# Moving fill tiles around the first attention's compressed scores, and reordering the second attention's vector, scalar and closing work

## The chip, the cores and the metric

The kernel runs on one core of a Trainium2 chip. The metric is the time of one execution on the device, in microseconds (us). Three timed runs of the kernel before gave 2184.55, 2186.37 and 2181.2 us, so the median is 2184.55 us.

## The reference

The reference is two transformer blocks applied one after the other to x, a 512 x 1024 float32 matrix, with all weights in float32. What matters here is cut out:

```python
# first block: "NSA" attention beside a convolution branch
u = rmsnorm(h, g_mix);  z = u @ w_in            # queries, keys, values, gates, conv input, merge gates
kc = compress(kv[0], ...); vc = compress(kv[1], ...)     # 31 compressed keys/values per group of heads
lc = q @ kc.T;  pc = masked_softmax(lc, cmp_end <= t);  o_c = pc @ vc
o_s, o_w = ...                                  # two causal softmax attentions over all 512 keys
o = gates[0] * o_c + gates[1] * o_s + gates[2] * o_w
h = h + (ga * (o @ w_o_nsa) + gb * conv_branch) @ w_out
... # gated feed-forward, per-layer embedding, norm

# second block, its first layer: "fox" attention with 16 heads of 64
s = q @ k.T + c[q] - c[k]        # c is a running sum of log_sigmoid(forget logits)
pr = softmax(causal(s));  o = pr @ v;  m = o @ w_attn_out
... # MLP, embedding, short convolution, MLP, embedding
```

With 512 positions all selection blocks are kept, so the selected attention and the window attention are both plain causal attention.

## The kernel before, in words

**Matrix products.** Every float32 product is made of three products of rounded parts (hi x hi, lo x hi, hi x lo), each a TensorE matmul of 128 x 128 weights on 512 columns. The weights come in "units" of 128 x 1024. SyncE's queue loads a unit, ScalarE rounds it (`w_hi`, L1855), GpSimd subtracts to get the low part (`w_lo`, L472), and TensorE multiplies. A unit is eight "tiles" of three matmuls (L519 to L521), and its eight tiles accumulate in one PSUM bank. VectorE then empties the bank and increments `bank_free`.

**Queues.** Each engine runs its own instruction list, in an order that is written out by hand. Semaphores tie the lists together. No planner is at work: an instruction that waits holds back all that stands behind it on its engine.

**First attention.** The function `fill(n)` makes the next n tiles of the 19 units in stage "pairs" (152 tiles). It is called between pieces of the attention, to keep TensorE at work while VectorE and ScalarE do the softmax. The table `NSA_FILL` says how many tiles go where. Its row j is a phase (there are nine), its column i a query block of 128 rows (there are four). In phase j and block i TensorE runs `scores(j, i)`, a first fill, the values product and the transposes (`turn`) of the phase before, and a second fill. Phases 0, 2, 4, 6 are the selected attention of head pairs 0 to 3, phases 1, 3, 5, 7 their window attention. The compressed scores of pair p are `cmp_scores(p)` (L752 and L758): two mask matmuls and 24 small ones of 64 rows and 32 columns, of which two with the same form follow each other. `cmp_scores(0)` stands ahead of everything else, the others at the end of phases 1, 3 and 5. Each of those waits for the exponentials of `scores(j, 3)`, since they share the PSUM banks 2 and 3.

VectorE answers block by block: the negated row maximum of the scores (`head_peaks`, L1339), then what is due of the fill units (`nsa_evict`), a step of the depthwise convolution (`taps(1)`, L1206 or L1209), the normalisation (`head_normalise`, L1343 and L1347), and another `taps(1)`. For the compressed scores it first takes maxima and subtracts (`cmp_peak`, L1378 and L1380). ScalarE does the exponentials (L2001). `scores` of a block waits for the exponentials of the block before it. `scores(j, 0)` of a new pair also waits for the subtraction of `cmp_peak`.

Ahead of the phases, VectorE copies the compressed keys and values from PSUM into `kc_f` and `vc_f` (L1307 to L1309), ScalarE rounds them, and VectorE subtracts to get `kc_lo` and `vc_lo` (L1149). TensorE waits for the latter before `cmp_scores(0)`.

**Second attention.** Eight pairs of heads run in the same style (`fox_pair`), with the table `FOX_FILL` and 24 tiles made ahead. Per pair TensorE runs four blocks of scores (L982, L984), turns v (L990), and then alternates transposes of the probabilities (L1000) with the values products (`pv`, L1007 to L1009). VectorE takes the maxima (`mx`, L1320), normalises (`nrm`, L1326 and L1329), makes the low parts of transposed probabilities (`lo`) and of the output (`out_low`, L1149), and empties fill units (`fox_evict`). The row `c_head` of the next pair is made by VectorE (L1652) after the last `nrm`. Pair 7 has no fill units left. Its fills are tiles of the output projection, whose bank must be empty first. The last group of that projection waits for the last `out_low`.

Of the kernel before, what the change touches and what calls it, by code (L numbers as in the profile page):

```python
# [17 lines left out]
P = 128  # L18
# [151 lines left out]
NSA_FILL = [((2, 2),) * 4] + [((2, 2),) * 4, ((2, 2, 2), (2, 1), (2, 2), (2, 1))] * 4  # L170
# [38 lines left out]
def build(nc, x_in, p_in, weights, vectors, last_gain, out):  # L209
# [4 lines left out]
    with ExitStack() as ctx:  # L214
# [59 lines left out]
        with ExitStack() as att:  # L274
# [4 lines left out]
            kc_f = sb("kc_f", [P, NCP], scope=att)  # L279
            kc_hi = sb("kc_hi", [P, NCP], F32R, att)  # L280
            kc_lo = sb("kc_lo", [P, NCP], F32R, att)
            vc_f = sb("vc_f", [2 * NC1, P], scope=att)
# [233 lines left out]
        def _(pe):  # L516
# [229 lines left out]
            def cmp_scores(p):  # L746
# [6 lines left out]
                for qi in range(QB):  # L753
                    qs = slice(qi * P, (qi + 1) * P)
                    for t, (q, k) in enumerate(((q_hi, kc_hi), (q_hi, kc_lo), (q_lo, kc_hi))):
                        for hd in range(2):
                            rows = slice(hd * HD, (hd + 1) * HD)
                            mm = pe.matmul(ps[:, 2 + hd, qi * NCP:(qi + 1) * NCP], q[rows, p % 2, qs], k[rows, :],  # L758
                                           start=False, stop=t == 2 and qi == QB - 1)
                mm.then_inc(s_cs["scores"], 1)  # L760
# [34 lines left out]

            pe.wait_ge(c_act, 5)
            pe.wait_ge(s_kv["lo"], 6)
            pe.wait_ge(s_kv["zero"], 4)
            pe.wait_ge(s_cmp["klo"], 2)
            for j in range(9):  # L800
                b = j - 1
                for i in range(QB):
                    pieces = NSA_FILL[j][i]
                    if j < 8:
                        if j == 0 and i == 0:
                            cmp_scores(0)
                            fill(pieces[0])
                        scores(j, i)
# [18 lines left out]
                    if j % 2 and i == QB - 1 and j < 7:  # L827
                        cmp_scores(j // 2 + 1)
# [203 lines left out]
            for p in range(8):  # L1032
                fox_pair(p)

# [104 lines left out]
        def _(dve):  # L1139
# [124 lines left out]
            dve.memset(kc_f[:], 0.0).then_inc(s_cmp["out"], 1)  # L1264
# [41 lines left out]
            dve.wait_ge(s_cmp["out"], 1)  # L1306
# [5 lines left out]
            dve.wait_ge(s_cmp["out"], 4)  # L1312
            low(kc_lo[:], kc_f[:], kc_hi[:], s_cmp["klo"])
            low(vc_lo[:], vc_f[:], vc_hi[:], s_cmp["klo"])
# [335 lines left out]
            def head_rows(p):  # L1650

                dve.tensor_scalar(c_head[:], c_rows[:], head_sel[:, p:p + 1], None, ALU.mult).then_inc(A2["crow"], 1)  # L1652

            head_rows(0)
# [14 lines left out]
            def fox_pair(p):  # L1669
# [14 lines left out]
                def out_low(hd):  # L1684
# [7 lines left out]
                mx(0); nrm(0); evict(0)  # L1692
# [6 lines left out]
                if p < 7:  # L1699
                    head_rows(p + 1)  # L1700
                evict(3)
                lo(0, 0); lo(0, 1); evict(4); lo(0, 2); evict(5); lo(0, 3); evict(6); lo(1, 0); out_low(0); lo(1, 1); evict(7)
# [795 lines left out]
```

## Time and profile before

| what | value |
|---|---|
| median of three runs | 2184.55 us |
| the profiled execution's own time | 2185.68 us |
| its span, first to last instruction | 2183.9 us |
| mean granted TensorE clock | 0.994 |
| TensorE busy | 2146.1 us, 98% of the span |
| VectorE, ScalarE, GpSimd busy | 46%, 40%, 43% |

TensorE's busy time counts a matmul as busy also when it runs at the lower clock. So the span less 2146.1 us is the time in which TensorE stood still, and time lost to the clock is inside the busy time. A timeline row gives start, duration, engine, line, operation, output and inputs, shapes and count, and in brackets how long the engine stood still before it and whose result it waited for. Consecutive matmuls overlap, so their pace is the difference of their starts, not their duration.

### The profile page before, as it was taken

The numbers are of one execution on the slowest core, as the hardware profiler recorded it, in microseconds if no ns is written. First come the engines' busy times: TensorE is split into PE (matmuls) and PEld (weight loads), VectorE is DVE, ScalarE is ACT, GpSimd is POOL, SyncE is SP. The second block draws the span as 40 slices with busy tenths as digits, with TensorE's granted clock in tenths as the row PEclk, the third lists the DMA queues.
The fourth block names the chain that finished last, engine by engine and source line by source line (L and its number), as shares of the span: only waits on it lengthen the run. The fifth ranks groups of instructions, "written<-read, shape, count | busy, mean of one in ns | idle before, by whom it ended". The sixth has DMA issues, their size and how long they took to land.

```text
span 2183.9 us, 25305 instructions
## 1 busy us (share of the span) xinstructions
PE 2146.1 (98%) x10192; PEld 1758.8 (81%) x10192; DVE 1013.6 (46%) x1637; ACT 869.6 (40%) x1358; POOL 933.8 (43%) x424
## 2 busy tenths in 40 slices
PE   9999999999999999999999999999999999999998
PEld 7877778888888887777778888888888888888886
DVE  5877775445524235666634422313653345122134
ACT  5434346444424254444434422324532244233234
POOL 5722124434444455322225444444554454444446
PEclk9999999999999999999999999999999999999999
DMA  4421112233233332211122333322223323332222
GB/s 159 148 75 41 47 49 80 94 97 106 97 97 97 97 115 78 70 57 49 49 67 88 97 97 97 97 97 87 97 87 97 97 85 99 97 97 96 97 80 85
DMA packets 53829, 193.27 MB, mean 88 GB/s; under 512 B 6096, under 2 KB 6224, under 8 KB 53712
## 3 DMA queue, kind: packets, MB, share of 16 engines
q1 hardware_dynamic: 52992, 189.81, 27.0%
q10 hardware_dynamic: 720, 1.84, 0.3%
q8 instruction: 81, 1.33, 0.2%
q14 instruction: 36, 0.29, 0.0%
HBM read 189.53 MB, written 2.10 MB: 88 GB/s over the span
## 4 chain that ended last, share of the span: by engine, by line
PE 89%; DVE 6%; ACT 3%; issue 1%; DMA 0%; POOL 0%; DVEq 0%; ACTq 0%; POOLq 0%
PE ps L519 27%; PE ps L521 27%; PE ps L520 27%; PE ps L733 1%; DVE ps L1209 1%; PE ps L982 1%; PE ps L713 1%; PE ps L1000 1%; PE ps L725 1%; ACT w_hi L1855 1%; PE ps L615 1%; DVE xg_lo L1169 1%; PE ps L1007 0%; DVE ps L1730 0%; PE ps L715 0%
## 5 line engine op out<-in xcount | busy, mean ns | idle before, releaser
L472 POOL TENSOR_TENSOR w_lo<-w_raw,w_hi 128x1024 fp32r<-128x1024 f32 x352 | 852.6, 2424 | 1211.4 <-ACT w_hi L1855 1211.3
L519 PE MATMUL ps<-xg_hi,w_hi 128*128 128x512 f32 x1688 | 674.1, 399 | 5.4 <-POOL w_lo L486 2.8
L521 PE MATMUL ps<-xg_hi,w_lo 128*128 128x512 f32 x1688 | 661.2, 392 | 0.0
L520 PE MATMUL ps<-xg_lo,w_hi 128*128 128x512 f32 x1688 | 660.7, 391 | 0.0
L1855 ACT ACTIVATE w_hi<-w_raw 128x1024 fp32r<-128x1024 f32 x352 | 372.3, 1058 | 626.5 <-PE ps L521 623.8
L519 PEld LDWEIGHTS ps<-xg_hi,w_hi 128*128 128x128 f32 x1688 | 318.8, 189 | 69.3 <-issue 3.0
L521 PEld LDWEIGHTS ps<-xg_hi,w_lo 128*128 128x128 f32 x1688 | 318.5, 189 | 67.9
L520 PEld LDWEIGHTS ps<-xg_lo,w_hi 128*128 128x128 f32 x1688 | 319.2, 189 | 59.4
L521 PE MATMUL ps<-h_hi,w_lo 128*128 128x512 f32 x688 | 267.8, 389 | 0.0
L519 PE MATMUL ps<-h_hi,w_hi 128*128 128x512 f32 x688 | 267.8, 389 | 0.0
L520 PE MATMUL ps<-h_lo,w_hi 128*128 128x512 f32 x688 | 267.8, 389 | 0.0
L1143 DVE TENSOR_TENSOR ps<-ps,inv_rms 128x512 f32<-128x512 f32 x164 | 113.6, 696 | 194.2 <-PE ps L521 181.1
L521 PEld LDWEIGHTS ps<-h_hi,w_lo 128*128 128x128 f32 x688 | 129.2, 188 | 26.9
L520 PEld LDWEIGHTS ps<-h_lo,w_hi 128*128 128x128 f32 x688 | 129.2, 188 | 26.7
L519 PEld LDWEIGHTS ps<-h_hi,w_hi 128*128 128x128 f32 x688 | 129.2, 188 | 26.6
L1499 DVE TENSOR_TENSOR mixed<-mixed,ps 128x512 f32<-128x512 f32 x48 | 33.0, 688 | 199.9 <-PE ps L521 199.9
L1169 DVE SCALAR_TENSOR_TENSOR xg_lo<-resid,vec,xg_hi 128x512 fp32r<-128x512 f32 x72 | 85.5, 1191 | 12.7 <-ACT xg_hi L1881 12.5
L1209 DVE SCALAR_TENSOR_TENSOR ps<-glu,vec,ps 128x512 f32<-128x512 f32 x116 | 87.1, 751 | 1.9
L1844 ACT ACTIVATE h_hi<-ps 128x512 fp32r<-128x512 f32 x86 | 51.5, 598 | 90.1 <-DVE ps L1761 48.8
L1881 ACT ACTIVATE xg_hi<-resid,vec 128x512 fp32r<-128x512 f32 x72 | 51.7, 717 | 62.7 <-DVE resid L1499 40.2
L481 POOL TENSOR_TENSOR sq_sum<-sq_sum,sq 128x512 f32<-128x512 f32 x42 | 66.2, 1577 | 23.7 <-ACT sq L1878 21.4
L1761 DVE TENSOR_TENSOR ps<-tile_b,ps 128x512 f32<-128x512 f32 x64 | 44.6, 696 | 57.7 <-ACT tile_b L2296 57.7
(342 smaller groups left out, 2462.7 us busy)
## 6 DMA issues: line engine op xcount, KB each, us to landing
w_raw<-in_weights SPq DMA_DIRECT2D x352, 512.0 KB, 3.5
out_x<-mixed SPq DMA_DIRECT2D x8, 256.0 KB, 2.1
resid<-in_x SPq DMA_DIRECT2D x3, 512.0 KB, 7.4
p_raw<-in_p ACTq DMA_DIRECT2D x3, 512.0 KB, 3.6
resid<-in_x SPq DMA_DIRECT2D x2, 256.0 KB, 4.0
last_gain<-in_last_gain SPq DMA_DIRECT2D x1, 512.0 KB, 4.6
w_raw<-in_weights SPq DMA_DIRECT2D x1, 256.0 KB, 4.0
w_raw<-in_weights ACTq DMA_DIRECT2D x1, 256.0 KB, 4.4
```

The lines of the kernel that those rows point to most:

```text
L472: pool.tensor_tensor(w_lo[:, slot, :], w_raw[:, u % RAW, :], w_hi[:, slot, :].bitcast(F32), ALU.subtract).then_inc(w_ready, 1)
L481: pool.tensor_tensor(sq_sum[:], sq_sum[:], sq[:, m % 2:m % 2 + 1, :], ALU.add).then_inc(summed, 1)
L519: pe.matmul(o, w, x, start=start, stop=False)
L520: pe.matmul(o, w, xl, start=False, stop=False)
L521: return pe.matmul(o, wl, x, start=False, stop=stop)
L1143: dve.tensor_tensor(out, ps[:, BANK[u]:BANK[u] + 1, :], R[:], ALU.mult).then_inc(done, 1)
L1169: dve.scalar_tensor_tensor(xg_lo[:, m:m + 1, :], X[:, m:m + 1, :], g, xg_hi[:, m:m + 1, :].bitcast(F32), ALU.mult, ALU.subtract).then_inc( ...
L1209: ins = dve.scalar_tensor_tensor(acc if k < CONV_TAPS - 1 else conv_acc[:, ct, :], src, w, acc, ALU.mult, ALU.add)
L1761: dve.tensor_tensor(t, T2[:, m % 2:m % 2 + 1, :], t, ALU.mult).then_inc(s_mlp["s"], 1)
L1844: act.activation(out, x, ACT.Copy, scale=scale).then_inc(done, 1)
L1855: act.activation(w_hi[:, u % RING, :], w_raw[:, u % RAW, :], ACT.Copy).then_inc(w_hi_ready, 1)
L1881: act.activation(xg_hi[:, m:m + 1, :], X[:, m:m + 1, :], ACT.Copy, scale=g).then_inc(prep_hi, 1)
```

## The change

The fill tables of phase 0 and of the odd phases are different. `cmp_scores` takes a list of fills to put between its four query blocks. Four tiles are made ahead of the wait for the compressed keys. `kc_f` and `vc_f` are gone: ScalarE and VectorE read the compressed keys and values from PSUM. In the second attention, the first maxima of a pair go ahead of the last low part and the last `fox_evict` of the pair before, `c_head` is made by ScalarE after its last exponentials, and six matmuls whose product nobody reads stand behind the last pair.

```diff
-NSA_FILL = [((2, 2),) * 4] + [((2, 2),) * 4, ((2, 2, 2), (2, 1), (2, 2), (2, 1))] * 4
+NSA_FILL = [((7, 2), (2, 0), (2, 0), (2, 1))] + [((2, 2), (2, 2), (2, 2), (1, 2, 1)), ((2, 2, 2), (2, 1), (2, 2), (2, 1))] * 4
...
-            def cmp_scores(p):
+            def cmp_scores(p, between):
...
                             mm = pe.matmul(ps[:, 2 + hd, qi * NCP:(qi + 1) * NCP], q[rows, p % 2, qs], k[rows, :],
                                            start=False, stop=t == 2 and qi == QB - 1)
+                    if qi < QB - 1 and between[qi]:
+                        fill(between[qi])
...
+            fill(4)
             pe.wait_ge(c_act, 5)
...
-            pe.wait_ge(s_cmp["klo"], 2)
+            pe.wait_ge(s_cmp["klo"], 4)
...
                         if j == 0 and i == 0:
-                            cmp_scores(0)
-                            fill(pieces[0])
+                            cmp_scores(0, (1, 1, 1))
                         scores(j, i)
...
                     if j % 2 and i == QB - 1 and j < 7:
-                        cmp_scores(j // 2 + 1)
+                        cmp_scores(j // 2 + 1, (0, pieces[2], 0))
+                    elif j == 7 and i == QB - 1:
+                        fill(pieces[2])
                     fill(pieces[1])
...
             for p in range(8):
                 fox_pair(p)
+            for _ in range(6):
+                pe.matmul(ps[:, 2, :], ident_r[:], ident_r[:].unsqueeze(1).to_broadcast([P, QB, P]), start=True, stop=True)
... # VectorE
-            dve.memset(kc_f[:], 0.0).then_inc(s_cmp["out"], 1)
+            for t in (kc_hi, kc_lo):
+                dve.tensor_scalar(t[:, NC1:NCP], ones[:, 0:1], 0.0, None, ALU.mult).then_inc(s_cmp["out"], 1)
...
-            dve.tensor_copy(kc_f[0:HD, 0:NC1], ps[0:HD, 4, 0:NC1]).then_inc(s_cmp["out"], 1)
-            dve.tensor_copy(kc_f[HD:P, 0:NC1], ps[HD:P, 4, NC1:2 * NC1]).then_inc(s_cmp["out"], 1)
-            dve.tensor_tensor(vc_f[:], ps[0:2 * NC1, 5, 0:P], own[:], ALU.mult).then_inc(s_cmp["out"], 1)
+            dve.tensor_tensor(ps[0:2 * NC1, 5, 0:P], ps[0:2 * NC1, 5, 0:P], own[:], ALU.mult).then_inc(s_cmp["out"], 1)
...
-            low(kc_lo[:], kc_f[:], kc_hi[:], s_cmp["klo"])
-            low(vc_lo[:], vc_f[:], vc_hi[:], s_cmp["klo"])
+            for g in range(2):
+                rows = slice(g * HD, (g + 1) * HD)
+                low(kc_lo[rows, 0:NC1], ps[rows, 4, g * NC1:(g + 1) * NC1], kc_hi[rows, 0:NC1], s_cmp["klo"])
+            dve.wait_ge(s_cmp["khi"], 3)
+            dve.tensor_tensor(vc_lo[:], ps[0:2 * NC1, 5, 0:P], vc_hi[:].bitcast(F32), ALU.subtract).then_inc(s_cmp["klo"], 2)
...
-                mx(0); nrm(0); evict(0)
+                mx(0)
+                if p:
+                    out_low(p - 1, 1)
+                    fox_evict(p - 1, 11)
+                nrm(0); evict(0)
...
                 mx(3); nrm(3)
-                if p < 7:
-                    head_rows(p + 1)
                 evict(3)
...
-                lo(1, 2); evict(8); lo(1, 3); evict(9); evict(10); out_low(1); evict(11)
+                lo(1, 2); evict(8); lo(1, 3); evict(9); evict(10)
+                if p == 7:
+                    out_low(7, 1)
... # ScalarE
-            act.wait_ge(s_cmp["out"], 4)
-            copy_hi(kc_hi[:], kc_f[:], s_cmp["khi"])
-            copy_hi(vc_hi[:], vc_f[:], s_cmp["khi"])
+            act.wait_ge(unit_done, U["cmp_out"] + 1)
+            for g in range(2):
+                rows = slice(g * HD, (g + 1) * HD)
+                copy_hi(kc_hi[rows, 0:NC1], ps[rows, 4, g * NC1:(g + 1) * NC1], s_cmp["khi"])
+            act.wait_ge(s_cmp["out"], 3)
+            copy_hi(vc_hi[:], ps[0:2 * NC1, 5, 0:P], s_cmp["khi"])
...
-                evict(1); ex(2); evict(2); ex(3); evict(3)
+                evict(1); ex(2); evict(2); ex(3)
+                if p < 7:
+                    act.activation(c_head[:], c_rows[:], ACT.Copy, scale=head_sel[:, p + 1:p + 2]).then_inc(A2["crow"], 1)
+                evict(3)
```

## Rows read from the trace of the kernel before

**Rows 1.** Waits of TensorE over the span: total us, times, longest us.
```profile
PE ps L752 <- DVE vc_lo L1149: 4.1, 1, 4.1
...
PE ps L752 <- ACT prob_w L2001: 1.6, 3, 0.5
```

**Rows 2.** Windows: length, busy by engine, then granted clock, DMA share, GB/s.
```profile
125.00:140.00 15.00, 12.17 (x61) 9.50 (x62) 7.34 (x13) 4.30 (x8) 2.44 (x2) 0.66 0.19 72
170.00:180.00 10.00, 9.48 (x64) 7.64 (x63) 5.36 (x14) 3.83 (x12) 0.92 (x1) 0.83 0.10 39
215.00:225.00 10.00, 9.48 (x70) 7.43 (x69) 7.11 (x14) 2.90 (x11) 1.64 (x1) 1.00 0.17 54
265.00:275.00 10.00, 9.48 (x67) 7.75 (x66) 6.38 (x15) 3.94 (x12) 0.36 (x1) 0.83 0.13 52
1110.00:1120.00 10.00, 8.12 (x31) 6.42 (x32) 4.55 (x9) 4.69 (x8) 3.01 (x2) 0.83 0.12 37
```

**Rows 3.** Timeline of TensorE, start of the first attention: start, duration, instruction.
```profile
123.16 0.39 PE L520 MATMUL ps<-xg_lo,w_hi 128*128 128x512 f32 x1
123.39 0.39 PE L521 MATMUL ps<-xg_hi,w_lo 128*128 128x512 f32 x1
127.83 0.41 PE L752 MATMUL ps<-cmp_mask_r,ident_r 128*128 128x128 f32 x2 [4.06 <-DVE vc_lo L1149]
...
131.75 0.63 PE L521 MATMUL ps<-xg_hi,w_lo 128*128 128x512 f32 x1
132.18 0.63 PE L519 MATMUL ps<-xg_hi,w_hi 128*128 128x512 f32 x1
```

**Rows 4.** Timeline of GpSimd beside it.
```profile
122.77 4.67 POOL L472 TENSOR_TENSOR w_lo<-w_raw,w_hi 128x1024 fp32r<-128x1024 f32 x2 [2.34 <-ACT w_hi L1855]
```

**Rows 5.** Timeline of VectorE, from the compressed keys to phase 1.
```profile
121.84 0.75 DVE L1149 TENSOR_TENSOR vv_lo<-ps,vv_hi 128x256 fp32r<-128x256 f32 x2
...
125.11 2.47 DVE L1149 TENSOR_TENSOR vc_lo<-vc_f,vc_hi 62x128 fp32r<-62x128 f32 x1
...
131.30 0.42 DVE L1380 TENSOR_TENSOR prob_c<-ps,c_stat 128x248 f32<-128x248 f32 x1
135.15 0.43 DVE L1339 TENSOR_REDUCE stat<-ps 128x2 f32<-128x256 f32 x1 [3.44 <-PE ps L715]
...
139.54 0.69 DVE L1339 TENSOR_REDUCE stat<-ps 128x2 f32<-128x512 f32 x1 [1.31 <-PE ps L715]
...
150.96 0.17 DVE L1343 RECIPROCAL stat<-stat 128x2 f32<-128x2 f32 x1 [0.25 <-ACT prob_s L2001]
...
152.74 0.42 DVE L1339 TENSOR_REDUCE stat<-ps 128x2 f32<-128x256 f32 x1
```

**Rows 6.** Window over phase 0 on VectorE's side, columns as above.
```profile
135.10:152.70 17.60, 16.93 (x83) 12.38 (x83) 15.49 (x33) 5.94 (x18) 2.39 (x1) 0.90 0.09 26
```

**Rows 7.** Timeline of TensorE at the second compressed scores.
```profile
170.94 0.41 PE L752 MATMUL ps<-cmp_mask_r,ident_r 128*128 128x128 f32 x2 [0.52 <-ACT prob_w L2001]
...
172.72 0.80 PE L519 MATMUL ps<-xg_hi,w_hi 128*128 128x512 f32 x1
```

**Rows 8.** Timeline of TensorE: pair 5, the start and the end of pair 7.
```profile
1038.28 0.39 PE L982 MATMUL ps<-fk_hi,fq_hi 64*128 64x256 f32 x2 [1.30 <-ACT fprob L1991]
...
1089.87 0.47 PE L519 MATMUL ps<-fo_hi,w_hi 128*128 128x512 f32 x1 [0.51 <-DVE fv L1143]
...
1114.78 0.79 PE L519 MATMUL ps<-fo_hi,w_hi 128*128 128x512 f32 x1 [1.41 <-DVE fo_lo L1149]
```

**Rows 9.** Timeline of VectorE at the same places, and c_head of pair 1.
```profile
914.91 0.48 DVE L1652 TENSOR_SCALAR c_head<-c_rows,head_sel 128x512 fp32r<-128x512 f32 x1
...
1037.11 0.48 DVE L1320 TENSOR_REDUCE fstat<-ps 128x1 f32<-128x128 f32 x2
...
1088.30 0.69 DVE L1149 TENSOR_TENSOR fo_lo<-ps,fo_hi 64x512 fp32r<-64x512 f32 x1 [2.06 <-ACT fo_hi L1844]
1089.03 0.69 DVE L1143 TENSOR_TENSOR fv<-ps,inv_rms 128x512 f32<-128x512 f32 x1
```

More of the change, by code:

```diff
@@ L1305, in _ @@
             dve.wait_ge(unit_done, U["cmp_out"] + 1)
-            dve.wait_ge(s_cmp["out"], 1)
-            dve.tensor_copy(kc_f[0:HD, 0:NC1], ps[0:HD, 4, 0:NC1]).then_inc(s_cmp["out"], 1)
-            dve.tensor_copy(kc_f[HD:P, 0:NC1], ps[HD:P, 4, NC1:2 * NC1]).then_inc(s_cmp["out"], 1)
-            dve.tensor_tensor(vc_f[:], ps[0:2 * NC1, 5, 0:P], own[:], ALU.mult).then_inc(s_cmp["out"], 1)
+            dve.tensor_tensor(ps[0:2 * NC1, 5, 0:P], ps[0:2 * NC1, 5, 0:P], own[:], ALU.mult).then_inc(s_cmp["out"], 1)
             dve.memset(token[:, 12:13], 0.0).then_inc(bank_free, 1)
             dve.wait_ge(s_cmp["khi"], 2)
-            dve.wait_ge(s_cmp["out"], 4)
-            low(kc_lo[:], kc_f[:], kc_hi[:], s_cmp["klo"])
-            low(vc_lo[:], vc_f[:], vc_hi[:], s_cmp["klo"])
+            for g in range(2):
[3 more added lines that the diff above has]
+            dve.tensor_tensor(vc_lo[:], ps[0:2 * NC1, 5, 0:P], vc_hi[:].bitcast(F32), ALU.subtract).then_inc(s_cmp["klo"], 2)
             dve.wait_ge(s_kv["lo"], 2)
@@ L1648, in _ @@
             dve.wait_ge(s_fg["dve"], 6)
-            def head_rows(p):
-                dve.tensor_scalar(c_head[:], c_rows[:], head_sel[:, p:p + 1], None, ALU.mult).then_inc(A2["crow"], 1)
-            head_rows(0)
+            dve.tensor_scalar(c_head[:], c_rows[:], head_sel[:, 0:1], None, ALU.mult).then_inc(A2["crow"], 1)
             counted = [3, 3]
@@ L1682, in lo, with out_low @@
                     split_turned(A2, e0 + 4 * hd + kb, kb % 2, (fpt_hi, fpt_lo), kb)
-                def out_low(hd):
+                def out_low(p, hd):
                     rows = slice(hd * HD, (hd + 1) * HD)
@@ L1698, in fox_pair @@
                 mx(3); nrm(3)
-                if p < 7:
-                    head_rows(p + 1)
                 evict(3)
-                lo(0, 0); lo(0, 1); evict(4); lo(0, 2); evict(5); lo(0, 3); evict(6); lo(1, 0); out_low(0); lo(1, 1); evict(7)
-                lo(1, 2); evict(8); lo(1, 3); evict(9); evict(10); out_low(1); evict(11)
+                lo(0, 0); lo(0, 1); evict(4); lo(0, 2); evict(5); lo(0, 3); evict(6); lo(1, 0); out_low(p, 0); lo(1, 1); evict(7)
+                lo(1, 2); evict(8); lo(1, 3); evict(9); evict(10)
+                if p == 7:
+                    out_low(7, 1)
             while counted[0] < 5:
```

2 lines of the change are left out of this document (removed).

## The prediction

> **What bounds the kernel now.** I read the page first: TensorE is busy for 2146.1 us of a span of 2183.9, so 38 us of standing still is all that filling can win back. What the clock costs comes on top, since a matmul at the lower clock counts as busy. Then I read the waits of TensorE. One wait stands out in the first attention: 4.06 us ahead of the first compressed scores, for `vc_lo` [rows 1, 3]. Three waits of 0.5 us stand ahead of the later ones. Then I read the granted clock in short windows. A window loses its length times (1 less the clock): 15 x 0.34 = 5.1 us behind the first compressed scores, 10 x 0.17 = 1.7 us at the second, nothing at the third, 1.7 us at the fourth, and 1.7 us at the end of the second attention [rows 2]. There the granted clock goes from 2.4 to 1.2 GHz: matmuls on 512 columns start 0.43 us apart instead of 0.23 [rows 3]. At these places TensorE had stood still or run the small matmuls. A tile (three matmuls) costs 0.69 us at the full clock. Last I read VectorE's timeline through phase 0, since TensorE's next scores wait for its maxima [rows 5, 6].
>
> **Part A: start of the first attention.** (1) The compressed keys. VectorE is free for them at 122.6, when the two low parts from 121.84 end. These two read PSUM on 256 elements each and took 0.75 us together [rows 5]. The new low parts read PSUM too and are smaller. A product in PSUM, three roundings by ScalarE beside it and three low parts come to about 1.2 us (estimate from those rows), so they are there at 123.8. TensorE ends the unit in front at 123.6 and then has four tiles, 2.75 us, until 126.4. The wait of 4.06 us is gone. In the kernel before, `vc_lo` took 2.47 us for 128 elements, while GpSimd ran from 122.77 to 127.44 [rows 4, 5]. If the new ones were stretched in the same way they would end at about 127.4, and a wait of 1 us would stay. I take zero, by the nearer row, that of `vv_lo`.
>
> The Trainium skill (SBUF — State Buffer, "Who interferes with whom") says that a tensor_tensor of VectorE with both inputs in SBUF contends with GpSimd's reads for a port pair. The long `vc_lo` agrees with it. By this rule the new form, with one input in PSUM, isn't held up. The sum is the same by the rule as by the row of `vv_lo`.
>
> (2) Compressed scores. They took 172.72 - 170.94 = 1.78 us at the full clock [rows 7]. Three tiles between them add 3 x 0.69, and I add 0.2 us a tile for the changes of shape (an estimate; 0 to 0.3). So they end at about 126.4 + 4.4 = 130.9.
>
> (3) A new wait. `scores(0, 0)` now stands directly behind them, with no tiles to cover VectorE's maxima and subtraction, two instructions of 0.42 us [rows 5]. TensorE waits about 1.1 us, and the first scores are done at about 132.9. VectorE took them up at 135.15 [rows 5]. That is 2.25 us gained, not the 9.2 us of idle time and clock.
>
> (4) Phase 0 belongs to VectorE. From 135.15 to its maxima for phase 1 at 152.74 it needs 17.6 us, of which it works 15.49 [rows 5, 6]. Its list isn't made shorter. Its wait of 1.31 us for the second scores goes, since these come at the full clock and behind two tiles instead of four; so does 0.2 us for the gates. Its wait for the last exponentials (0.25 us at 150.96) grows by 0.6, since `query_low` now comes a block earlier and no longer covers it. So 16.7 us from 132.9: it reaches phase 1 at 149.5 instead of 152.74, 3.2 us earlier.
>
> (5) TensorE's side. Behind the first scores it has nine tiles left instead of fourteen, and some 10 us of work in 16.7 us. It stands still, with one piece of about 3.5 us ahead of `scores(0, 3)`: the maxima of block 2 come only after VectorE's longest block (convolution, compressed normalisation, a query unit). A standstill of 4.06 us was followed by the lower clock until about 138.6 [rows 2, 3]. So I expect it here too, over `scores(0, 3)` and the three tiles behind it. They then need about 5.5 us, while VectorE's exponentials leave 4. TensorE comes to phase 1 1.3 us later than VectorE would let it. Part A: -3.2 + 1.3 = **-1.9 us**. Bounds: -3.6 with no fall of the clock, -0.5 if the clock falls behind the compressed scores as well.
>
> **Part B: the other compressed scores.** One tile goes from in front of them to between them. But the wait in front is for exponentials whose time is set by `scores(j, 3)`, and this wait was already open, 0.52 us each time [rows 1, 7]. TensorE comes 0.69 us earlier and waits 0.69 us more: 3 x 0.69 = +2.1 us. The tile between has a change of shape more: 3 x 0.2 = +0.6 us (0 to 0.9). Clock: the stretch without a tile ahead of the first tile is as long as before (1.2 us of waiting and half of the small matmuls, against 0.5 and all of them), and the other half follows soon. I expect two falls in three, as before [rows 2]. Bounds: none (-3.4) to three (+1.7). Part B: **+2.7 us**.
>
> **Part C: order and `c_head` in the second attention.** Pair 5: TensorE waits 1.30 us for exponentials whose maxima VectorE began at 1037.11, behind the low part and a fill unit [rows 8, 9]. In front they begin about 1.5 us earlier: **-1.3 us**. Pair 7 goes the other way: its first fill needs the bank that VectorE empties into `fv`, and TensorE waited 0.51 us for it [rows 8]. Before, VectorE did `fo_lo` at 1088.30 and `fv` at 1089.03, ahead of the maxima. Now the maxima come first and wait for the scores (done at about 1089.1), so it is 1089.1 + 0.5 maxima + 0.65 `fo_lo` + 0.7 `fv` = 1091.0 instead of 1089.72 [rows 9]. What is queued behind the fill, the second scores, follows: **+1.3 us**. In other pairs, `fo_lo` now stands between maxima and normalisation and delays the list by some 0.3 us. That shows where a later wait is open (pairs 3 and 6): **+0.5 us** (0 to 0.8). `c_head` leaves VectorE, 0.48 us [rows 9]. It helps in pairs 0 and 1, where a low part of the probabilities is awaited behind it; on ScalarE it takes about 0.6 us, mostly in idle time. **-0.4 us** (-0.9 to +0.6).
>
> **Part D: unread products.** Six matmuls of 0.23 us are 1.4 us, and the wait for the last low part is 1.41 us [rows 8]. They fill it and delay nothing (0 to +0.1). They don't shorten it. What they can save is the clock behind it: **-1.7 us** [rows 2], bounds 0 and -1.7.
>
> **Sum.** -1.9 + 2.7 - 1.3 + 1.3 + 0.5 - 0.4 - 1.7 = -0.8 us. The profiled execution took 2185.68 us, so the same would take 2184.9. It was 1.1 us above the median of the runs shown. The median then becomes 2184.55 - 0.8 = 2183.7 us.
>
> **Rivals.** (a) The filling does what its place suggests. VectorE isn't the bound of phase 0, because its list closes up, or the clock stays full, and most of the 4.1 + 5.1 us is won, less the new wait of 1.1 us. For it: the two waits that TensorE has on VectorE's side in phase 0 were short. Against it: VectorE works 15.49 of 17.6 us there [rows 6], and its work isn't less. Part A -8 instead of -1.9: 2177.6 us.
>
> (b) The tile between the small matmuls keeps the clock at 2.4 GHz in part B. For it: at the third compressed scores, with the same idle time, the clock stayed [rows 2], so little decides it. Against it: the waiting ahead of it grows. -3.4: 2180.3 us.
>
> (c) Slower: TensorE's added standstills bring the lower clock wherever they lie. It falls behind the first compressed scores too (+1.4), at all three later ones (+1.7), and behind the wait of 1.8 us at the start of pair 7 (+1.7): -0.8 + 4.8 = +4.0, so 2188.6 us. It decides from the point where a standstill and the small matmuls beside it have no tile among them for as long as at the second compressed scores. Part B's stretches are at that point.
>
> (d) The reordering of pair 5 finds that the wait has moved elsewhere: +1.3, inside the forecast's own range.
>
> **How the numbers follow.** The forecast has 0.52 (with d), (a) 0.20, (b) 0.16, (c) 0.12. The bound of what can be told apart is 0.2%, 4.4 us: 2180.2 and 2188.9. (a) is faster than that, (b) in half of its cases, (c) slower in most; the forecast itself hardly ever. So 0.28 faster, 0.62 no change, 0.10 slower. The range takes in (a) and most of (c): 2177 to 2188.
>
> **What would show it.** Part A: the wait of L752 for `vc_lo` is gone, a wait of about 1 us stands ahead of the first L713 (for `prob_c`), and one of 3 to 4 us ahead of the fourth. The maxima of phase 1 come about 3 us earlier. Part B: three waits of 1.2 us for `prob_w`. Part C: no wait at the start of pair 5, 1.8 us for `fv` at the start of pair 7. Part D: clock 1.00 behind the last pair. I am wrong if TensorE has no long wait in phase 0, or if the windows at the compressed scores all show a clock of 1.00.

## The result: slower by 0.3%, and the profile after

The changed kernel takes **2192.0 us** (median of 20 runs, 2185.4 to 2197.0); the kernel before takes 2184.8 us beside it (20 runs, 2181.2 to 2187.2). The ratio is 1.0030, with a 95% interval of 1.0022 to 1.0037: slower by 6.6 us. (The medians are 7.2 us apart. The ratios in this document are taken over all runs, and lie up to 0.0007 from the quotient of the medians.) I had forecast 2183.7 and a range up to 2188. The prediction is wrong in direction, and the median lies outside its range. Over its 20 runs, time goes with the granted clock: the six of 2185.4 to 2186.4 us had a mean clock of 0.996 to 0.997, the eight above 2194 had 0.990 to 0.991. But even those six are not below the median of the kernel before, so the clock is not all of it. One execution of an experiment below, 2564.9 us at a mean clock of 0.781 in `e13_b_three_behind`, stands apart from all others and is left out of its ratio.

The profiled execution took 2193.31 us, its span is 2191.6 (before: 2185.68 and 2183.9). First the page and the waits of TensorE (total us, times, longest us).

```profile
PE 2152.3 (98%) x10198; PEld 1761.5 (80%) x10198; DVE 1007.2 (46%) x1630; ACT 873.9 (40%) x1366; POOL 933.5 (43%) x424
```

```profile
PE ps L711 <- ACT prob_s L2008: 5.7, 2, 5.3
PE ps L750 <- ACT prob_w L2008: 3.6, 3, 1.2
PE ps L984 <- ACT fprob L1998: 3.4, 6, 1.4
...
PE ps L517 <- DVE fv L1147: 2.0, 1, 2.0
...
PE ps L711 <- DVE prob_c L1384: 1.0, 1, 1.0
```

The wait for `vc_lo` [rows 1] is gone; it has become 1.0 us for `prob_c` and 5.3 us for exponentials later in the same phase. The three waits of L750 have grown from 0.5 to 1.2 us each. Busy time grew by 6.2 us, of which the six added products are 1.4 us. The remaining 4.8 us are about what the mean granted clock gives (0.994 before, 0.992 now, 4.4 us). Where the lower clock lies, the windows show (length, busy by engine, then granted clock, DMA share, GB/s).

```profile
118.00:150.00 32.00, 25.31 (x134) 18.73 (x133) 21.81 (x44) 12.94 (x29) 9.22 (x4) 0.95 0.22 66
160.00:190.00 30.00, 28.79 (x151) 22.19 (x150) 17.00 (x30) 8.69 (x21) 4.75 (x2) 0.83 0.11 36
210.00:240.00 30.00, 28.78 (x161) 22.04 (x160) 18.82 (x36) 10.00 (x24) 4.79 (x2) 0.89 0.16 53
255.00:285.00 30.00, 28.79 (x166) 22.77 (x165) 21.46 (x41) 12.40 (x31) 5.34 (x3) 0.89 0.10 36
1105.00:1135.00 30.00, 27.70 (x138) 21.81 (x137) 12.92 (x27) 11.78 (x24) 6.98 (x3) 1.00 0.13 36
```

The three middle windows are those around the later compressed scores. They lose 30 x (0.17 + 0.11 + 0.11) = **11.7 us** of full clock; the same three places lost 1.7 + 0 + 1.7 before [rows 2]. That is 8.3 us more, which is as large as the whole loss of this execution. At the first compressed scores it is the other way round, 1.6 us lost in the first window against 5.1 [rows 2], and behind the last pair nothing against 1.7. So the clock costs 3.1 us more in these five places together.

The start of the attention, on VectorE (start, duration, instruction, idle time before and its releaser):

```profile
122.66 0.41 DVE L1153 TENSOR_TENSOR kc_lo<-ps,kc_hi 64x31 fp32r<-64x31 f32 x2 [0.16 <-ACT kc_hi L1848]
123.10 0.28 DVE L1318 TENSOR_TENSOR vc_lo<-ps,vc_hi 62x128 fp32r<-62x128 f32 x1
...
132.69 0.43 DVE L1343 TENSOR_REDUCE stat<-ps 128x2 f32<-128x256 f32 x1 [1.01 <-PE ps L713]
...
138.49 2.49 DVE L1399 TENSOR_TENSOR prob_c<-prob_c,c_stat 128x248 f32<-128x248 f32 x1
...
152.10 0.42 DVE L1343 TENSOR_REDUCE stat<-ps 128x2 f32<-128x256 f32 x1
```

The same stretch on GpSimd, and on TensorE:

```profile
122.43 4.74 POOL L470 TENSOR_TENSOR w_lo<-w_raw,w_hi 128x1024 fp32r<-128x1024 f32 x2 [2.33 <-ACT w_hi L1859]
138.32 2.38 POOL L470 TENSOR_TENSOR w_lo<-w_raw,w_hi 128x1024 fp32r<-128x1024 f32 x1 [11.15 <-ACT w_hi L1859]
```

```profile
131.73 0.33 PE L711 MATMUL ps<-kk_hi,q_hi 64*128 64x128 f32 x2 [0.96 <-DVE prob_c L1384]
...
145.28 0.80 PE L711 MATMUL ps<-kk_hi,q_hi 64*128 64x512 f32 x2 [5.32 <-ACT prob_s L2008]
...
170.31 0.41 PE L750 MATMUL ps<-cmp_mask_r,ident_r 128*128 128x128 f32 x2 [1.21 <-ACT prob_w L2008]
...
171.99 0.39 PE L519 MATMUL ps<-xg_hi,w_lo 128*128 128x512 f32 x1
...
172.77 0.38 PE L756 MATMUL ps<-kc_hi,q_hi 64*128 64x32 f32 x2
...
173.51 0.79 PE L517 MATMUL ps<-xg_hi,w_hi 128*128 128x512 f32 x1
174.10 0.63 PE L518 MATMUL ps<-xg_lo,w_hi 128*128 128x512 f32 x1
...
182.23 0.73 PE L517 MATMUL ps<-xg_hi,w_hi 128*128 128x512 f32 x1
182.81 0.40 PE L518 MATMUL ps<-xg_lo,w_hi 128*128 128x512 f32 x1
```

VectorE's first maxima come at 132.69 (135.15 before, [rows 5]), 2.46 us earlier, but its maxima for phase 1 only 0.64 us earlier (152.10 against 152.74). In between, one 128x248 product took 2.49 us, where the kernel before needed 0.42. GpSimd's product ran beside it, from 138.32 to 140.70. Then, behind the second compressed scores, matmuls on 512 columns start 0.43 us apart from 173.5 to 182.2; before, they were back at 0.23 us by 176.6.

At the start of pair 7, TensorE waits for `fv`, which VectorE makes behind maxima and `fo_lo` (VectorE's timeline):

```profile
1097.06 0.49 DVE L1324 TENSOR_REDUCE fstat<-ps 128x1 f32<-128x128 f32 x2 [3.04 <-PE ps L986]
1097.58 0.69 DVE L1153 TENSOR_TENSOR fo_lo<-ps,fo_hi 64x512 fp32r<-64x512 f32 x1
1098.31 0.69 DVE L1147 TENSOR_TENSOR fv<-ps,inv_rms 128x512 f32<-128x512 f32 x1
```

Now the account over the whole span, which is 7.7 us longer. The mask of the second compressed scores starts at 170.31, against 170.94 before: -0.63 us up to there, or -1.3 without B's longer wait (0.7). B then gives 2.5 us of waits and changes of shape (worked out below) and 8.3 us of clock. The second attention and the end must give the rest, -1.8 us.

### The profile page after: what moved, and what is told of

The parts are those of the page before. It is cut to its first block, busy times and chain, and to the rows that moved or that the text cites. A ratio compares the mean times of both kernels' runs of the same rounds, so it can differ in the third digit from the quotient of the medians.

```text
span 2191.6 us, 25317 instructions
## 1 busy us (share of the span) xinstructions
PE 2152.3 (98%) x10198; PEld 1761.5 (80%) x10198; DVE 1007.2 (46%) x1630; ACT 873.9 (40%) x1366; POOL 933.5 (43%) x424
## 4 chain that ended last, share of the span: by engine, by line
PE 92%; DVE 4%; ACT 3%; issue 1%; DMA 0%; POOL 0%; DVEq 0%; ACTq 0%; POOLq 0%
PE ps L517 28%; PE ps L519 27%; PE ps L518 27%; PE ps L731 1%; PE ps L984 1%; PE ps L711 1%; PE ps L723 1%; PE ps L1002 1%; PE ps L613 1%; DVE xg_lo L1173 1%; ACT w_hi L1859 1%; PE ps L713 1%; PE ps L1009 0%; DVE ps L1734 0%; PE ps L1011 0%
```

## The experiments

Each was timed 5 to 12 times, beside 9 to 35 runs of the kernel before on the same chip. The letters are the prediction's: A the start of the first attention, B the later compressed scores, C and D the second attention. Ratios are to the kernel before; 0.0010 is 2.2 us.

**Which part costs.** `e1_no_b` is the changed kernel with the old tiles at the later compressed scores:

```diff
-..., (2, 2), (2, 2), (1, 2, 1)), ...   # 1 ahead, 1 between, 2 behind
+..., (2, 2), (2, 2), (2, 2)), ...      # 2 ahead, 2 behind
```

> The changed kernel with part B taken back (odd phases of NSA_FILL are (2, 2) four times again, no tile between the later compressed scores); all else as changed. Theory 1 (part B's tile between the small matmuls keeps the clock low for two or three times as long as before: 12.0 us lost in the windows from 150 to 300 us, against 3.4): the time falls by about 10 us from the changed kernel's 2192, to 2182, the waits for prob_w go back from 1.2 to 0.5 us, and the runs lie within some 5 us as before. Theory 2 (the new start, part A, shifts the attention so that the clock falls longer at its later places): little changes, 2189 or more, and the windows still lose 8 us or more.

`e2_b_only` is the kernel before with only that line changed (and the tile between):

> The kernel before with part B alone (odd phases end in (1, 2, 1), one tile between the second and third query block of the later compressed scores). Theory 1: about 10 us slower than before, 2194, spread over some 10 us from run to run; waits of 1.2 us for prob_w three times, and the granted clock about 0.90 to 0.93 in the 50 us windows around them. Theory 2: only the predicted 2.7 us slower, 2187.5, with the clock about as before.

`e3_fox_only` has C and D alone, on the kernel before:

> The kernel before with parts C and D alone (maxima in front, c_head by ScalarE, six unread products). Both theories: 1.8 us faster than before (pair 5 -1.3, pair 7 +1.5, c_head -0.6, clock behind the last pair -1.7, the rest +0.3), 2183. If the unread products don't save the clock, 2184.7.

`e4_front_only` has A alone: the shorter chain of the compressed keys, `fill(4)` in front of the attention, one tile in each gap of the first compressed scores, and the first row of the table.

> The kernel before with part A alone (four tiles in front, three between the first compressed scores, no kc_f and vc_f). Theory 1: 0 to 1 us faster than before, 2184.3: the 9 us at the start turn into a wait of 5.3 us ahead of the fourth scores and a shorter fall of the clock. VectorE's product prob_c takes about 2.5 us while GpSimd works. Theory 2: slower than before by several us, with falls of the clock at the later compressed scores that the kernel before doesn't have.

Measured: `e1_no_b` 2185.9 us, ratio 1.0013 (1.0004 to 1.0023); `e2_b_only` 2190.2, 1.0031 (1.0019 to 1.0044); `e3_fox_only` 2183.9, 1.0001 (0.9988 to 1.0014); `e4_front_only` 2186.8, 1.0017 (1.0009 to 1.0026); the kernel before 2182.2. So B costs 6.8 us by itself and is the part that costs most; taken out of the changed kernel it gives back 3.7 us (1.0030 - 1.0013), not the 10 us that the profiled execution had suggested. That one execution had drawn long stretches of lower clock at all three places. A costs 3.7 us where I had forecast a gain of 1.9 (0 to 1 just ahead of this run), and C with D is worth nothing where I had forecast -1.6 (-1.8 ahead of this run). Summed, the parts alone give 10.7 us, more than the 6.6 of the whole; each has some 2 to 3 us of interval to either side.

The kernel before was itself faster beside these four (2182.2 us) than beside all others (2185.0 to 2185.6), while the kernel with B alone was not: it took 2190.2 us here and 2189.4 when it was timed again on the same chip (`e15_b_again`, below). So these four ratios may be too high by up to 0.0013, or 2.9 us, and A's cost lies between 2.0 us (its 2186.8 less the 2184.8 of the result) and 3.7. One source of such a difference stands in the trace of `e3_fox_only`, whose start of the first attention is that of the kernel before, unchanged (VectorE's timeline):

```profile
125.04 0.28 DVE L1151 TENSOR_TENSOR vc_lo<-vc_f,vc_hi 62x128 fp32r<-62x128 f32 x1
...
147.46 0.42 DVE L1341 TENSOR_REDUCE stat<-ps 128x2 f32<-128x256 f32 x1
```

Here `vc_lo` took 0.28 us instead of 2.47, TensorE waited 1.9 us for it instead of 4.1, and VectorE reached phase 1 at 147.46 instead of 152.74. The one trace of the kernel before is of the long kind. That the faster runs of the kernel before are of the short kind is not shown.

**What in A.** `e5_chain_only` keeps only the shorter chain of the compressed keys. The table and TensorE's program stay as before:

```diff
-dve.tensor_copy(kc_f..., ps...); dve.tensor_copy(kc_f..., ps...); dve.tensor_tensor(vc_f[:], ps..., own[:], ALU.mult)
+dve.tensor_tensor(ps[0:2 * NC1, 5, 0:P], ps[0:2 * NC1, 5, 0:P], own[:], ALU.mult)
...
-low(kc_lo[:], kc_f[:], kc_hi[:], ...); low(vc_lo[:], vc_f[:], vc_hi[:], ...)
+low(kc_lo[rows, 0:NC1], ps[rows, 4, ...], ...)   # twice
+dve.tensor_tensor(vc_lo[:], ps[0:2 * NC1, 5, 0:P], vc_hi[:].bitcast(F32), ALU.subtract)
```

> The kernel before with nothing but the shorter way to kc_lo and vc_lo (kc_f and vc_f gone, both read from PSUM); the fill table is the old one, so no tiles stand in front and none between the compressed scores. Theory 1 (phase 0 is set by VectorE's list, so what counts is how early the first scores are there; tiles in front only delay it): TensorE goes on at 123.8 instead of 127.8 with the clock at 1.00, VectorE's first maxima come at about 127.7 instead of 135.15, those of phase 1 at about 145 instead of 152.7, and the time falls by 7 us (0.9968). Theory 2 (tiles must fill the start, or the clock falls there): the clock still falls behind the bare compressed scores, and no more than 3 us are won.

`e7_late_query` is `e4_front_only` with one difference: VectorE and ScalarE take the query unit of phase 0 one block later, as the kernel before did.

```diff
-nsa_evict(nsa_made(j, i - 1) if i else ...)
+nsa_evict(0 if (j, i) == (0, 1) else nsa_made(j, i - 1) if i else ...)
```

> The kernel with part A alone (e4), but ScalarE and VectorE take up the first finished query unit one block later, as the kernel before did. Theory 1 (part A ended slower than forecast since the query unit's weights come earlier, GpSimd's w_lo then runs beside VectorE's SBUF-only product prob_c and holds it up): prob_c takes 0.42 us instead of 2.49, TensorE's wait ahead of the fourth scores shrinks from 5.3 to about 2.7 us, and the time falls by 2 to 3 us from e4. Rival (the long wait comes from the length of VectorE's list alone): the wait stays above 4.5 us.

Measured: `e5_chain_only` **2175.4 us, 0.9956 (0.9943 to 0.9968)**, 9.6 us faster than before; `e7_late_query` 2182.7, 0.9990 (0.9981 to 0.9999). VectorE's timeline in `e5_chain_only`:

```profile
128.04 0.43 DVE L1337 TENSOR_REDUCE stat<-ps 128x2 f32<-128x256 f32 x1 [1.55 <-PE ps L713]
...
133.26 0.42 DVE L1393 TENSOR_TENSOR prob_c<-prob_c,c_stat 128x248 f32<-128x248 f32 x1
...
144.12 0.42 DVE L1337 TENSOR_REDUCE stat<-ps 128x2 f32<-128x256 f32 x1
```

and in `e7_late_query`:

```profile
133.72 0.43 DVE L1339 TENSOR_REDUCE stat<-ps 128x2 f32<-128x256 f32 x1 [1.01 <-PE ps L713]
...
138.94 0.42 DVE L1395 TENSOR_TENSOR prob_c<-prob_c,c_stat 128x248 f32<-128x248 f32 x1
...
149.79 0.42 DVE L1339 TENSOR_REDUCE stat<-ps 128x2 f32<-128x256 f32 x1
```

GpSimd's next product came behind `prob_c` in `e7_late_query`, not beside it:

```profile
144.62 2.40 POOL L470 TENSOR_TENSOR w_lo<-w_raw,w_hi 128x1024 fp32r<-128x1024 f32 x1 [16.41 <-ACT w_hi L1855]
```

From the first maxima to those of phase 1 VectorE needs 144.12 - 128.04 = 16.08 us in the one and 149.79 - 133.72 = 16.07 us in the other. So phase 0 has a length of its own, with the old tiles in it as with the new ones. In the changed kernel it is 19.41 us, because of the 2.49 us of `prob_c` and what shifts behind it. And its start has moved from 128.04 to 132.69: 2.3 us for the tiles put in front of the compressed scores, and three tiles between them. Together, 4.65 + 3.33 = 8.0 us lie between 144.12 and 152.10.

TensorE's wait ahead of the fourth scores is 2.66 us in `e7_late_query`, as expected (2.7). The time fell by 5.9 us by ratio, or 4.1 by the medians, where I had expected 2 to 3. What I had left out is the clock: in 118:150 it was 0.85 in `e4_front_only` and is 1.00 in `e7_late_query`, which is 4.8 us.

TensorE's clock at the start of the attention in `e5_chain_only` is full:

```profile
120.00:160.00 40.00, 39.12 (x227) 29.94 (x226) 32.71 (x69) 20.39 (x47) 12.09 (x6) 1.00 0.22 67
```

against 0.87 in the kernel before for the same 40 us: the shorter chain took away the standstill, and with it the 5.1 us of lower clock [rows 2].

**Which half of B.** `e6_tile_between` has the tile in the middle of the small matmuls without the longer wait (2 ahead, 1 between, 1 behind); `e9_tile_behind` has the longer wait without a tile between (1 ahead, 3 behind). `e13_b_three_behind` and `e14_b_last_quarter` vary B itself (three tiles behind instead of two; the tile ahead of the last quarter of the small matmuls instead of in their middle), `e15_b_again` repeats it.

```diff
-(2, 2)       # before: 2 ahead, 2 behind
+(2, 1, 1)    # e6_tile_between
+(1, 3)       # e9_tile_behind
+(1, 3, 1)    # e13_b_three_behind; the next block's (2, 2, 2) becomes (1, 2, 2)
```

> The kernel before with one tile between the second and third query block of the later compressed scores, taken from behind them, not from in front ((2, 1, 1)). If the wait in front makes the clock fall long (theory W): waits stay at 0.5 us, and the time is 0 to 1 us above the kernel before. If the tile between does it (theory T: at 1.2 GHz small matmuls and single tiles don't raise the clock again): 4 to 6 us slower.

> The kernel before with one tile moved from in front of the later compressed scores to behind them ((1, 3)), none between. Waits of 1.2 us for prob_w three times, +2.1 us. Theory W: the clock falls at all three places, and the time is 5 us or more above the kernel before. Theory T: 2 to 3 us above it, since three tiles behind them raise the clock as before.

> Only the later compressed scores, one tile ahead and one between as in the change, but three behind instead of two (the third is taken from behind the next block's first scores). Without the clock the edit costs 3 x 0.8 = 2.5 us. Theory 1 (after a standstill, small matmuls and a single tile, two tiles and the next block's small scores are too little to bring the clock back, so it stays low for two stretches instead of one): with three tiles it comes back sooner, the remaining 4 us of the edit's cost go, ratio about 1.0010 to 1.0015. Rival (the split itself decides, what stands behind does not matter): as the edit alone, 1.0031.

> Only the later compressed scores, one tile ahead, the single tile before the last quarter of the small matmuls instead of in their middle, two behind. Theory 1 (too few tiles behind the last small matmuls): as the edit alone or slightly less, 1.0025 to 1.0031. Rival (the second half of the small matmuls, 0.7 to 1.3 us without a tile, renews the fall): a quarter is too short for it, so about 1.0013, as with the wait alone.

> The change's tiles at the later compressed scores and nothing else, once more, for a second trace and a figure on the same chip. Theory 1: 1.0031 again, with a lower granted clock than before, and in its trace two or three falls at 170 to 285 us, some of them of about 7 us or more. Rival (the first figure was an accident of that call): 1.0012, the waits and changes of shape alone.

Measured: `e6_tile_between` 1.0003 (0.9994 to 1.0011), `e9_tile_behind` 1.0006 (0.9997 to 1.0015), `e13_b_three_behind` 1.0026 (1.0012 to 1.0040), `e14_b_last_quarter` 1.0032 (1.0020 to 1.0044), `e15_b_again` 1.0018 (1.0009 to 1.0026). The clock around the second compressed scores, in `e15_b_again`:

```profile
160.00:190.00 30.00, 28.75 (x151) 22.15 (x150) 16.76 (x30) 8.83 (x20) 4.75 (x2) 0.83 0.12 40
```

in `e9_tile_behind`:

```profile
160.00:190.00 30.00, 28.76 (x170) 22.13 (x169) 19.64 (x39) 10.40 (x25) 4.78 (x2) 0.94 0.12 36
```

and in `e6_tile_between`:

```profile
160.00:190.00 30.00, 29.46 (x165) 22.76 (x163) 19.11 (x38) 10.01 (x24) 4.78 (x2) 0.89 0.12 36
```

The start of the mask gives the cost without the clock. From the second to the fourth compressed scores it is 95.55 us before (170.94 to 266.49), 96.99 in `e9_tile_behind`, 97.78 in `e6_tile_between` and 100.59 in `e15_b_again`. Less what the clock lost in between (1.7, 1.8, 3.3 and 5.1 us), these are 93.8, 95.2, 94.5 and 95.5 us. For each of the two places in between: 0.7 us for the wait, 0.3 us for the tile's changes of shape, 0.8 us for both. I had forecast 0.7, 0.2 and 0.9. So that part of the step was right, 2.5 us for three places, and B's other 1.2 to 4.3 us (its four figures below) are to be put down to the clock. Each half alone costs 0.7 to 1.3 us in all, so both theories of one half fail: theory W wanted 5 us or more from `e9_tile_behind`, theory T 4 to 6 us from `e6_tile_between`. `e14_b_last_quarter` rules out that the length of the second lot of small matmuls matters: at a quarter of them the cost is as high (7.0 us). `e13_b_three_behind` decides nothing; its interval reaches from one theory to the other. `e15_b_again` came at 3.9 us, and its interval holds the rival's 1.0012 and not the 1.0031 of the first time; in its trace one long fall stands (5.1 us) where I had expected two or three. On its own it leaves B's cost between 2 and 6 us.

**Does B's cost hang on the rest, and what is the best of both?** `e8_chain_fox` has the shorter chain with `c_head` on ScalarE, the unread products, and the maxima in front in pairs 1 to 6 only; `e10_chain_after_fox` has the second attention exactly as changed. `e16_best_with_b` puts B into `e8_chain_fox`.

```diff
 mx(0)
-if p:              # changed kernel, e10_chain_after_fox
+if 0 < p < 7:      # e8_chain_fox
     out_low(p - 1, 1)
     fox_evict(p - 1, 11)
```

> The kernel before with the shorter chain of the compressed keys (alone 0.9956, -9.6 us), ScalarE's c_head, the six unread products, and the second attention's maxima in front in pairs 1 to 6; pair 7 keeps the order of before, so that its fv is not behind maxima and fo_lo. Theory 1 (the second attention's part came out at +0.2 us instead of -1.8 because of pair 7's wait of 2.0 us and the lower clock that follows it in some executions): pair 5 -1.3, c_head -0.4, other pairs +0.5, the end's clock -1.7, together -2.9 beside the chain's -9.6: -12.5 us, ratio 0.9943; pair 7 waits 0.5 us for fv. Rival (the reordering in the other pairs, or unread products that give no clock back, eat it): no more than -1 beside the chain's: -10.6 us or less, ratio 0.9952 or more.

> The same with the second attention exactly as in the changed kernel, pair 7's order too. Theory 1 (pair 7's order costs about 1.3 us of waiting and 1.7 us of lower clock in some executions): -9.6 + 0.2 = -9.4 us, ratio 0.9957, some 2 to 3 us above the kernel with pair 7's old order; pair 7 waits 2.0 us for fv. Rival (pair 7's order is not what ate the gain): within 1 us of that kernel.

> The fastest kernel (chain, c_head, unread products, maxima in front in pairs 1 to 6; 0.9943) with the change's tiles at the later compressed scores. Theory 1 (the cost lies at the place): +6.8 us on 0.9943, ratio 0.9974, less by up to 2 us if falls that were there anyway are only moved. Rival (the clock term hangs on the 15 us at the lower clock ahead of it at the first compressed scores, which the chain removes): only the 2.5 us of waits and changes of shape, 0.9954.

Measured: `e8_chain_fox` **2173.2 us, 0.9943 (0.9929 to 0.9956)**, the fastest of all; `e10_chain_after_fox` 2176.4, 0.9959 (0.9946 to 0.9971); `e16_best_with_b` 2179.9, 0.9974 (0.9964 to 0.9985). All three came out as theory 1 had them. Pair 7's order costs 3.2 us on one chip. Its wait in `e8_chain_fox`, on TensorE's timeline:

```profile
1076.10 0.47 PE L517 MATMUL ps<-fo_hi,w_hi 128*128 128x512 f32 x1 [0.52 <-DVE fv L1143]
```

The window around pair 7 there:

```profile
1060.00:1100.00 40.00, 36.83 (x211) 28.76 (x211) 22.65 (x53) 18.10 (x45) 4.79 (x2) 1.00 0.09 27
```

and in `e10_chain_after_fox`, where the wait is 2.0 us:

```profile
1060.00:1100.00 40.00, 36.41 (x194) 28.50 (x192) 20.18 (x48) 15.65 (x39) 4.75 (x2) 0.91 0.09 27
```

In `e16_best_with_b` nothing at the lower clock lies between 118 us and the later compressed scores, and B costs 6.8 us all the same. Its second and third windows:

```profile
210.00:240.00 30.00, 28.76 (x158) 22.02 (x157) 19.18 (x39) 9.86 (x24) 4.76 (x2) 0.89 0.11 35
255.00:285.00 30.00, 28.75 (x161) 22.18 (x160) 19.00 (x39) 10.48 (x25) 4.76 (x2) 0.89 0.13 36
```

while in `e8_chain_fox` the same windows, without B, are full:

```profile
210.00:240.00 30.00, 29.92 (x188) 23.78 (x189) 23.12 (x48) 11.79 (x30) 4.78 (x2) 1.00 0.12 36
255.00:285.00 30.00, 29.46 (x187) 23.16 (x186) 22.66 (x47) 11.50 (x30) 4.79 (x2) 1.00 0.15 51
```

**More tiles ahead.** `e11_chain_three_ahead` is `e5_chain_only`, and `e12_chain_fox_three` is `e8_chain_fox`, with the table moved the other way:

```diff
-(2, 2)    # 2 ahead of the compressed scores, 2 behind
+(3, 1)    # 3 ahead, 1 behind
```

> The kernel before with the shorter chain, and at the three later compressed scores one tile moved from behind them to in front (3 ahead, 1 behind), the opposite of the change. Theory 1 (waiting just ahead of the small matmuls is what drops the clock): the waits of 0.52 us for prob_w are gone, three times 0.17 us are added, and the falls of the clock there go: +0.5 - 3.4 = -2.9 us beside the chain's -9.6, -12.5 us, ratio 0.9943. Rival (few tiles behind the small matmuls keep the clock low for longer, whatever stands ahead): the clock falls behind them and with one tile there stays low for longer, +0.5 to +4: -9.1 to -5.6 us, ratio 0.9958 to 0.9974.

> The chain, the second attention with pair 7's old order, and three tiles ahead, one behind at the later compressed scores. Theory 1: -9.6 - 2.9 - 2.9 = -15.4 us, ratio 0.9930. Rival for the tiles: -12.5 + 0.5 to 4 = -12 to -8.5 us, ratio 0.9945 to 0.9961. The parts lie at different places of the program and should add.

Measured: 2176.4 us, 0.9958 (0.9946 to 0.9971), and 2174.1 us, 0.9945 (0.9933 to 0.9958). Both are where the same kernels with two tiles ahead are (0.9956, 0.9943). The waits of 0.5 us went, as forecast, but the clock still fell behind two of the three compressed scores (0.94 in 210:240 and in 255:285). So a wait ahead of the small matmuls isn't needed for a fall. A shorter one was left behind them: with one tile there, TensorE waits 0.2 us for `prob_c` in all three places, and where it falls the lower clock begins within 1 us behind that wait.

```profile
212.21 0.33 PE L711 MATMUL ps<-kk_hi,q_hi 64*128 64x128 f32 x2 [0.23 <-DVE prob_c L1378]
```

Theory 1 of these two was wrong, and there is nothing to win by it.

## Why the prediction was wrong

**Two steps failed: step 4 of Part A, "So 16.7 us from 132.9", and the clock term of Part B, "I expect two falls in three, as before".** By the parts timed alone, A came out 5.6 us above its forecast (3.7 against -1.9), B 4.1 us above it in `e2_b_only` and 2.6 by the average of its four figures, and C with D 1.8. Taken out of the changed kernel the other way round, A, C and D together cost 2.8 us (`e1_no_b`) against a forecast of -3.5, which is 6.3 us off, and B's 3.7 is only 1.0 us off. So step 4 is the larger miss, and B's is the one whose size is less certain.

**Part A** (forecast -1.9, measured +3.7 alone, or +2.0 by the medians): steps 1 to 3 came as written. The wait for `vc_lo` went (the low parts took 0.41 and 0.28 us), the first scores waited 0.96 us instead of 1.1, and the first maxima stood at 132.69 instead of 132.9. Then VectorE needed 19.41 us, not 16.7, to phase 1. The list itself is 16.1 us, as `e5_chain_only` and `e7_late_query` show, so it was slightly shorter than forecast. What I missed is that the query unit, taken a block earlier, lets ScalarE round the next weights earlier, which starts GpSimd's product right where VectorE scales `prob_c`. I had priced exactly this contention for `vc_lo`, and the Trainium skill names it (SBUF — State Buffer, "Who interferes with whom"); this trace agrees once more, with 2.49 us against 0.42. I looked for it where the change removed an operand pair and not where it moved a GpSimd instruction. `e7_late_query` moves it back, and 5.9 us by ratio (1.0017 to 0.9990) return. Part A then stands at -2.2 us, beside the forecast's -1.9. That the two are so close is partly luck: the standstill that I gave 3.5 us is 2.66 us there, and the fall of the clock that I had forecast for step 5 doesn't come. With the contention the standstill was 5.3 us, and the fall came with it.

**Part B.** The clock term was priced at nothing, with +1.7 us (a third fall) as its upper bound. The number of falls was the wrong thing to count, because a fall has no fixed length. Over the windows 160:190, 210:240 and 255:285 the eight traces without a change at these places lost 3.6, 3.3, 3.3, 3.3, 3.3, 5.1, 0 and 0 us (before, `e1`, `e3`, `e4`, `e5`, `e7`, `e8`, `e10`), 2.7 on average. The four with B lost 11.7, 5.1, 5.1 and 6.6 us (after, `e2`, `e15`, `e16`), 7.1 on average; the two variants of B lost 5.1 (`e14`) and 1.8 (`e13`), and all six 5.9. There was a fall at 8 of 24 places without B and at 9 of 18 with it, so the two falls in three of the one trace that I had were above the average of either. What grew is the price of one: 2.7 us without B, 3.9 with it. The single traces scatter, so the mean granted clock of all runs is the better witness. With B it is lower by 0.0014 (`e2` against before), 0.0011 (after against `e1`), 0.0007 (`e15` against before) and 0.0010 (`e16` against `e8`), which is 3.1, 2.4, 1.5 and 2.2 us, 2.3 on average; the halves `e6` and `e9` differ from before by 0.2 and -0.4 us. With the 2.5 us that I had worked out for waits and shapes, this makes 4.8. B's cost by timing is 6.8 (`e2`), 3.7 (after less `e1`), 3.9 (`e15`) and 6.8 us (`e16` less `e8`), 5.3 on average. So B costs about twice the +2.7 of the forecast, and most of the excess is clock. I had seen the rows that could have warned me: at the first compressed scores a fall had cost 5.1 us, not 1.7 [rows 2]. Why the wait and the tile are harmless one by one and not together, no run here shows. In the after trace the tile between still ran at full speed; the other half of the small matmuls, two tiles, the next block's short scores, two more tiles and the values product stood at half speed before the clock came back at 182. That too few long matmuls follow is argued from that, not shown, and `e13_b_three_behind`, made to show it, left it open.

More was in reach than I saw. Rival (a), -8 us on "the filling does what its place suggests", had the right size and the wrong cause: -9.6 us comes from the shorter chain with the **old** table. The tiles moved in front give 7.4 us of it back (`e7_late_query`, -2.2), and the contention 5.9 more (`e4_front_only`, +3.7). In phase 0 VectorE is the bound, and the tiles ahead of its first maxima delay it by 4.65 us; the other 2.7 us lie within the intervals of the two runs. The working did say that phase 0 belongs to VectorE. It didn't draw the consequence that the wait was best left unfilled.

**Part C**: pair 5's wait of 1.30 us is gone from the trace; pair 7's grew from 0.51 to 2.0 us (forecast 1.8); pairs 3 and 6 wait as much as before (0.56 us in pair 3 then, 0.26 twice now), so that the +0.5 didn't come; `c_head` leaves a wait of 0.48 us where 0.88 stood in pair 0. The undersized term is pair 7, forecast +1.3: 3.2 us by `e10` against `e8`. In the trace of `e10` the lower clock follows that wait (0.91 over 40 us, 3.6 us), as rival (c) had it for this place, and the mean clock of its runs is 0.9954 against 0.9970. It doesn't follow every time: it is there in three (`e1`, `e3`, `e10`) of the four traces with that wait, and not in that of the changed kernel. Behind the wait of 0.5 us of pair 7's old order no trace has it. **Part D**, forecast -1.7, was priced as if the fall behind the last pair came in every execution. With the unread products it came in none of the seven traces that have them. Without, it came in four of the eleven (before, `e5`, `e7`, `e11`), so the products are worth 1.7 x 4/11 = 0.6 us on average, and less if a fall is only put off: in `e8` and `e12` one came some 40 us later, beside a wait of 0.69 us of the next stage.

**Rival (c)** was the one that came, at 2188.6 us and a chance of 0.12. Its mechanism held at the later compressed scores and, in three traces of four, behind pair 7's wait, though the fall at the first compressed scores that it also counted did not come (1.00 in 125:140). It priced a fall at 1.7 us a place and kept Part A's 16.7 us, and even it was 3.4 us short.

## What to carry to other kernels

Before you fill a wait of the busiest engine, find out which engine's list sets the end of that phase: if it is another's, filler placed ahead of its first input delays the whole phase by about the filler's length (4.65 us here), and what paid was shortening the chain that ends in the wait (-9.6 us with the table untouched). A place where the clock fell in one trace is a place with a distribution: price it by several traces, with a longer fall as a bound, and time two edits of one place together, since the two that were harmless alone here were not so together. When an instruction moves, look at what it releases on the other engines and what that will run beside.

## What the runs showed of the hardware

- A stretch at the lower clock (1.2 GHz) had no fixed price. It lost 1.7, 3.3 or 5.1 us at places of the same code in different executions, and where none came it lost 0. Runs of the changed kernel spread over 11.7 us and those of the kernel before, beside them, over 6.0.
- A standstill ahead of the small matmuls wasn't needed for it: in `e11_chain_three_ahead` TensorE reached the compressed scores without waiting, and the clock was still 0.94 in two of three windows behind them, where the only wait was one of 0.2 us.
- VectorE's product of two operands in SBUF took 2.49 us instead of 0.42 in the three traces where GpSimd's weight product had begun just before it (after, `e1_no_b`, `e4_front_only`), and its low parts with one operand in PSUM took 0.28 to 0.41 us beside the same GpSimd instruction. In the after trace the long product began 0.17 us behind GpSimd's and ended 0.28 us behind its end (140.98 against 140.70).
- Which of the two is held up can go either way in the same code. The wait for the long `vc_lo` was 4.1 us in seven traces and 1.9 in that of `e3_fox_only`. There `vc_lo` began at 125.04, just as one GpSimd product gave way to the next, and took 0.28 us; GpSimd's second product took 2.50 us, where the same two took 2.35 and 2.37 in the kernel before.
